# A convolution tile's last group-statistics product, placed behind the first product of the next tile

## What is computed

```python
u = cg * xin
y = conv_b + conv_w[0]*u_pad[:, :-2] + conv_w[1]*u_pad[:, 1:-1] + conv_w[2]*u_pad[:, 2:]
a_out = _rmsnorm((bg * y).reshape(bsz, T, 8, 64), g_conv)
```

## Time and profile before

| | |
|---|---|
| median of three runs | 2019.57 us |
| the profiled execution, its own time | 2018.64 us |
| its span, first to last instruction | 2016.5 us |
| PE busy | 1990.5 us, 99% of the span |
| VectorE (DVE) busy | 887.8 us, 44% |
| ScalarE (ACT) busy | 493.9 us, 24% |
| GpSimd (POOL) busy | 96.3 us, 5% |
| granted TensorE clock, mean | 0.996 |
| the chain that ended last | PE 96%, DVE 2%, ACT 1% |

### The profile page before, as it was taken

How to read it: one execution, slowest core, us unless ns; L and a number is a source line. 1 busy time by engine, 2 the same in 40 slices (tenths; PEclk the granted TensorE clock), 3 DMA queues, 4 the chain that set the end, 5 groups by cost and what they waited for, 6 DMA issues and landing times.

```text
span 2016.5 us, 31170 instructions
## 1 busy us (share of the span) xinstructions
PE 1990.5 (99%) x12604; PEld 1977.3 (98%) x12604; DVE 887.8 (44%) x1541; ACT 493.9 (24%) x884; POOL 96.3 (5%) x151
## 2 busy tenths in 40 slices
PE   7999999999999999999999999999999999999998
PEld 7999999999999999999999999999999999999998
DVE  6524333343343338512677865433423432343344
ACT  6202211221112124333444523212211121121022
POOL 1000000000000013100000022000000000000001
PEclk9999999999999999999999999999999999999999
DMA  6012201210121012211111332011101110110102
GB/s 212 21 43 63 62 21 42 62 62 21 42 62 50 12 51 69 76 42 42 32 32 32 123 84 64 21 43 63 62 16 46 62 38 24 62 62 21 52 1 86
DMA packets 144178, 105.10 MB, mean 52 GB/s; under 512 B 6376, under 2 KB 136248, under 8 KB 144120
## 3 DMA queue, kind: packets, MB, share of 16 engines
q1 hardware_dynamic: 143992, 104.26, 16.8%
q10 hardware_dynamic: 128, 0.03, 0.0%
HBM read 95.36 MB, written 8.92 MB: 52 GB/s over the span
## 4 chain that ended last, share of the span: by engine, by line
PE 96%; DVE 2%; ACT 1%; issue 0%; ACTq 0%; DVEq 0%; POOL 0%
PE bank L201 31%; PE bank L206 30%; PE bank L207 30%; PE bank L205 1%; PE bank L203 1%; PE bank L2038 0%; PE bank L2052 0%; PE bank L2051 0%; ACT in_lo L757 0%; PE bank L886 0%; PE bank L2054 0%; PE bank L142 0%; PE bank L2081 0%; PE bank L2017 0%; DVE conv_out L1810 0%
## 5 line engine op out<-in xcount | busy, mean ns | idle before, releaser
L201 PE MATMUL bank<-in_hi,w_hi 128*128 128x352 f32 x2256 | 736.8, 327 | 4.9 <-DVE in_lo L736 3.7
L207 PE MATMUL bank<-in_hi,w_lo 128*128 128x352 f32 x2256 | 725.8, 322 | 0.0
L206 PE MATMUL bank<-in_lo,w_hi 128*128 128x352 f32 x2256 | 725.4, 322 | 0.0
L201 PEld LDWEIGHTS bank<-in_hi,w_hi 128*128 128x128 f32 x2256 | 424.9, 188 | 8.4 <-issue 3.9
L206 PEld LDWEIGHTS bank<-in_lo,w_hi 128*128 128x128 f32 x2256 | 426.1, 189 | 1.0
L207 PEld LDWEIGHTS bank<-in_hi,w_lo 128*128 128x128 f32 x2256 | 425.0, 188 | 0.0
L406 DVE TENSOR_TENSOR ffn_hidden<-ffn_silu,bank 128x352 f32<-128x352 f32 x132 | 68.8, 521 | 659.4 <-PE bank L207 579.1
L201 PE MATMUL bank<-ffn_hidden_hi,ffn_w_hi_more 128*128 128x352 f32 x1056 | 340.6, 323 | 0.0
L417 DVE SCALAR_TENSOR_TENSOR x<-bank,x 128x352 f32<-128x352 f32 x528 | 266.4, 524 | 154.4 <-PE bank L207 106.9
L206 PE MATMUL bank<-ffn_hidden_lo,ffn_w_hi_more 128*128 128x352 f32 x924 | 296.7, 321 | 0.0
L207 PE MATMUL bank<-ffn_hidden_hi,ffn_w_lo_more 128*128 128x352 f32 x924 | 296.7, 321 | 0.0
(11 more groups left out here) (225 smaller groups left out, 1483.8 us busy)
## 6 DMA issues: line engine op xcount, KB each, us to landing
raw<-in_ffn_w_gate SPq DMA_DIRECT2D x44, 512.0 KB, 3.9
ffn_raw_more<-in_ffn_w_down SPq DMA_DIRECT2D x44, 512.0 KB, 5.6
raw<-in_w_in SPq DMA_DIRECT2D x24, 512.0 KB, 3.9
raw<-in_ffn_w_up SPq DMA_DIRECT2D x22, 512.0 KB, 5.0
ffn_raw_more<-in_ffn_w_up SPq DMA_DIRECT2D x22, 512.0 KB, 5.6
x_parked<-x SPq DMA_DIRECT2D x3, 1408.0 KB, 7.1
x<-x_parked SPq DMA_DIRECT2D x3, 1408.0 KB, 10.8
raw<-in_w_out SPq DMA_DIRECT2D x8, 512.0 KB, 3.8
```

Of the source, the lines that this page charges most:

```text
L201: pe.matmul(out, w_hi, in_hi, start=first, stop=False)
L206: pe.matmul(out, w_hi, in_lo, start=False, stop=False)
L207: return pe.matmul(out, w_lo, in_hi, start=False, stop=last)
```

## The change

The third `stats` of a tile leaves the tile's end. In the tiles 1 to 3 TensorE now issues it, for the tile before, behind cg(0) and ahead of stage_a(even). The last tile, which has no successor, keeps its own at its end. The condition that it waits for is the same count of `z_squared`. No instruction is added or removed, and the lists of VectorE, ScalarE, GpSimd and SyncE are as they were.

```diff
-            def conv_tile(c, first, _):
+            def conv_tile(c, first, last):
...
-                def stats(b):
-                    pe.wait_ge(s.z_squared, c * 3 + (b + 1))
+                def stats(b, behind=0):
+                    pe.wait_ge(s.z_squared, c * 3 + (b + 1 - 3 * behind))
                     pe.matmul(dense[b][:, 0:BLK], sh.mean_group[:, :], rows[:, CONV_SQ, block_columns(b)],
                               start=True, stop=True).then_inc(s.group_stats, 1)
 
                 pe.wait_ge(m.w_low, c * 3 + (QKVO_TILES + 2))
                 cg(0)
+                if not first:
+                    stats(2, 1)
                 stage_a(even, c * (2 * CHUNK), CHUNK)
                 cg(1)
...
                 stats(0)
                 bg(2)
                 stats(1)
-                stats(2)
+                if last:
+                    stats(2)
```

## The result

The changed kernel took 2026.60 us as the median of 11 runs (2022.39 to 2028.20), the kernel before 2020.02 us (2018.63 to 2020.98, 11 runs on the same chip). By the medians that is 6.6 us more. The ratio over all these runs is 1.0030, about 6 us, with a 95% interval of 1.0022 to 1.0039, which is 4.4 to 7.9 us: slower, as forecast, and the 5.3 us of the sum lie inside that interval. A second set of five runs gave 2027.52 against 2019.53, 8.0 us. The chain of the prediction is found in the trace row by row; one term was missing in the profiled execution, and it is TensorE's clock.

A forecast was written before the change was run, and what follows sets the result against it. TensorE, busy 99% of the span, was taken to bound the kernel. Three tile ends losing 1.69, 1.71 and 1.92 us sum to 5.32 us, giving 2024.9 us against 2019.57; 80% range 2022.8 to 2026.3 us.

The forecast's parts named there:

- the 5.3 us of the sum: Total loss forecast over three changed tile ends: 1.69 + 1.71 + 1.92 = 5.32 us.
- The tile's end: At three tile ends PE's wait for the square becomes one for group_mean(0), about 0.7 us; cg(0) runs 0.51 us earlier.
- The third mean: VectorE's group_mean(2) follows stats(2) in its new place and comes 3.90 us later; stats(2) takes 0.76 us in the stream.
- The cushion: VectorE's 2.67 us idle before stage_c is used up by the 3.90 us delay; L1804 would be 1.14 us late.
- The rival by which the cushion holds: VectorE's 2.67 us idle time before stage_c swallows the delay; 2019.6 us, no slower; chance 0.08.
- stage_c: PE at L1947 must wait for h_normed, a new stall of 0.4 to 0.8 us, not added to the sum.
- PE's earlier arrival: At L2017 PE's earlier arrival is used up by the 0.4 to 0.8 us stall at L1947, so that stall is not added.
- GpSimd: Its delayed copies run into VectorE's L1801, which ends 1.10 us behind the last copy; 0.55 us of the 1.69 us lateness.
- The rival without contention: GpSimd's copies do not block VectorE's L1801; 3.67 us in all, 2023.2 us; chance 0.20.
- What follows is paced by PE, so the 1.69 us stay: Behind L2017, which comes 1.69 us later, PE sets the pace, so the loss stays in full.
- the sum's own range: Forecast time with the longer lag of stats(2) and the full price of GpSimd's copies: 2024.4 to 2026.0 us.
- More is late: A late state update opens a further wait on the numerators or ScalarE, 0.7 us a tile; about 2027 us; chance 0.10.

The follow-up runs named there:

- e2: Changed kernel with the third statistics in the middle of cg(0), behind four of its eight k-tiles; 2020.05 us, ratio 0.9998 to the kernel before.
- e3: Changed kernel with the last operation of VectorE's group norm (L1810) and the pad moved behind the state update; 2020.77 us, ratio 1.0000 to the kernel before.
- e4: Kernel before, with the last operation of VectorE's group norm (L1810) and the pad moved behind the state update; 2017.13 us, ratio 0.9984.
- e1: Changed kernel with GpSimd's copy of keys and values ahead of its two copies of queries; 2024.48 us, ratio 1.0019 to the kernel before.
- e7: Changed kernel plus nine unused matmuls ahead of the odd stage_a in each of tiles 1 to 3; 2025.10 us, ratio 1.0026 to the kernel before.
- e5: The changed kernel itself, run a second time beside other kernels; 2027.52 us, ratio 1.0035 to the kernel before.
- e6: Changed kernel with the third statistics one step further back, behind stage_a(even); 2032.06 us, ratio 1.0061 to the kernel before.
- e8: Kernel before, with the next even chunk's stage_a between stats(1) and stats(2), and VectorE's L1810 and pad behind the state update; 2014.58 us, ratio 0.9976.

## Why the prediction was right, and where it was short

**The tile's end.** Right. The wait for the square went from four to one, and a wait of 0.7 to 0.8 us for group_mean(0) took its place three times (2.2 us in all).

**The third mean.** 3.90 us late was forecast, 3.94 was measured; stats(2) took 0.75 us in the stream as in the earlier trace rows.

**The cushion.** Used up, as forecast: L1793 starts 1.19 us late from the mark (1.14 in the sum). The rival by which the cushion holds fails on the size of the delay alone. e2, with half of it, is that rival come true: no slower than before.

**stage_c.** The new wait at L1947 is 1.1 us over three tiles, 0.4 at most, against 0.4 to 0.8 each. That it is not to be added holds, since PE's wait at L2017 comes behind it and ends with L1764. "PE's earlier arrival" is right if it means ahead of L1764; earlier than in the kernel before PE is not, it reaches L1947 0.67 us late. Without the wait at L2017 the stall would count, as e3 beside e4 shows.

**GpSimd.** The forecast rested on one row with a cast of 1.95 us. Here it was a plain copy, and L1801 took 1.81 us and ended 1.11 us behind it (1.10 in the sum), in all three tiles. The Trainium skill's rule (SBUF — State Buffer, section Who interferes with whom), by which a VectorE instruction with two SBUF inputs contends with a GpSimd instruction that reads SBUF, is borne out by e1: with that copy out of the way the operation is back at 1.25 us. The rival without contention is out.

**The sum of the chain.** L1764 came later by 1.74 us in the second tile (from L1855: 23.83 us against 1019.20 - 997.11 = 22.09), and another 1.74 from there to the third tile's (50.99 against 49.25); with the third tile end e7 gives 5.44 us in all. Forecast: 1.69, 1.71 and 1.92, together 5.32.

**What was missing.** The step that failed is the sentence "What follows is paced by PE, so the 1.69 us stay". It takes PE's pace as given. In its place the runs showed that behind the longer waits PE's clock can fall to half for 3.5 to 7 us, at 1.6 us a fall, or twice that in e5; in e6, where PE had to wait for L1764 behind the fall anyway, it cost next to nothing. Medians 6.6 and 8.0 us over before, against a chain of 5.4, would leave 1.2 to 2.6 us to the clock. That is an estimate: the interval of either set also holds the chain alone, and the fall is shown by the profiled executions. The median of 2026.60 us lies above the sum's own range (to 2026.0) and just above the 80% range (to 2026.3); 0.45 us of that is the kernel before, which took 2020.02 us beside it and not 2019.57. "More is late", the rival at some 2027 us, named nearly this time, but by a further wait on the numerators or on ScalarE; no such wait is in the trace. The sum had no term for the clock, and the trace of before had a hint that I did not read. Ahead of the tiles PE does 31 tiny products (the 27 of the first row and four of 4x9), waits 1.09 us for L1701, and some 2 us later its clock falls:

```profile
915.73 1.72 PE L2003 MATMUL bank<-ident,mix_rows 4*32 4x4 f32 x27
...
918.99 0.61 PE L2017 MATMUL bank<-ident,mix_staged_kv 128*32 128x128 f32 x4 [1.09 <-DVE mix_decay L1701]
```

```profile
918.00:920.00 2.00, 1.01 (x9) 0.89 (x9) 0.91 (x4) 0.30 (x1) 0.00 (x0) 1.00 0.07 13
920.00:922.00 2.00, 2.00 (x18) 1.89 (x18) 0.89 (x3) 1.08 (x5) 0.80 (x2) 0.72 0.92 254
922.00:924.00 2.00, 2.00 (x8) 2.00 (x8) 0.00 (x0) 0.00 (x0) 0.82 (x1) 0.50 0.03 8
```

A wait is not the only thing that a fall can follow. In the same trace the clock falls again near 938 us with no wait of PE ahead of it, only 3.7 us of products with a side of 32 (933.85 to 937.60):

```profile
933.85 0.40 PE L2051 MATMUL bank<-mix_values,mix_probs 32*32 32x129 f32 x2
...
936.53 1.14 PE L2054 MATMUL bank<-mix_values,mix_keys 32*128 32x258 f32 x4
```

```profile
938.00:940.00 2.00, 2.00 (x9) 2.00 (x8) 1.90 (x8) 0.80 (x4) 0.00 (x0) 0.50 0.91 250
940.00:942.00 2.00, 2.00 (x11) 2.00 (x10) 0.63 (x3) 1.92 (x6) 0.00 (x0) 0.66 0.04 11
```

Nine of the ten traces have this second fall; e5's has none there, though the change's own, of the same kernel, has it. So part of the spread between executions has nothing to do with the change.

**What stays open.** That the falls inside the tiles hang on the long waits rests on one profile of each kernel, and all of them agree: the change twice and e6 have waits of 1.8 to 2.8 us and falls; e7 has the same lateness without the waits and no fall, and e1 to e4 and e8, whose waits are 1.3 us at most, have none. Why one such wait is followed by a fall and the next is not (the second tile of the change waited 1.83 us and kept its clock) no run here tells apart, nor why e5's fall lasted twice as long. How many falls an execution has I know from one profile each; the spread of the change's 11 runs, 2022.39 us at a mean clock of 0.997 to 2028.20 at 0.994, fits a number that changes, inside the tiles and outside.

## What to carry to other kernels

An instruction that leaves a waiting place frees nothing if the next one there is as late: look first at who else is late at the gap, then at what is queued behind the moved instruction's result, and compare its delay with the idle time (the cushion) of that engine before it is next needed; half the delay was free here, the whole of it cost 5.4 us. Fill a gap with work whose inputs are long there and delay the late chain by less than its cushion (2.75 us gained in e8), rather than move a link of that chain behind other work. And where a sum ends in longer waits of TensorE, look in the trace for places where its clock fell, behind a wait or behind small products, and put that price into the range where nothing later absorbs it.

## What the runs showed of the hardware

A wait of 1.9 us in an otherwise dense stream was followed by a granted clock of 0.50, for 3.5 us in one profile and for about 7 in another; the sum had taken 1.00 throughout, as in the tiles before. With nine matmuls of no use in each gap the clock stayed at 1.00 in the profile, and the kernel was 1.0 to 2.4 us faster by the medians than without them. In the kernel before, the clock also fell to 0.50 behind 3.7 us of products with a side of 32, with no wait at all. And a VectorE operation with both operands in SBUF that started 0.12 us behind a plain GpSimd copy of 0.82 us ended 1.11 us behind the copy's end: it took 1.81 us instead of 1.25, three times out of three.
